# Feed-forward stages' last chunk taken tile by tile, its second weights in the first weights' buffer; first tile's norm diagonal and the attentions' first product started earlier

## The reference, cut to what matters

```python
def rmsnorm(x, g):
    x32 = x.astype(jnp.float32)
    y = x32 * lax.rsqrt(jnp.mean(x32 * x32, axis=-1, keepdims=True) + EPS)
    return (y * g.astype(jnp.float32)).astype(x.dtype)

def swiglu(h, w_in, w_out):            # w_in 1024 x 5632, w_out 2816 x 1024
    gate, up = jnp.split(h @ w_in, 2, axis=-1)
    return (jax.nn.silu(gate) * up) @ w_out

x = x + 0.5 * swiglu(rmsnorm(x, norm_g[layer, 0]), ffn_w_in[layer, 0], ffn_w_out[layer, 0])
hn = rmsnorm(x, norm_g[layer, 1])
x = x + mixer(hn, ...)
x = x + 0.5 * swiglu(rmsnorm(x, norm_g[layer, 2]), ffn_w_in[layer, 1], ffn_w_out[layer, 1])
```

## Time and profile before

| | us |
|---|---|
| median of 3 runs | 2130.42 (2128.65 to 2131.54) |
| the profiled execution, its own time | 2131.05 |
| span of its trace | 2129.7 |
| TensorE busy (matmuls) | 2080.2 |
| VectorE busy | 1197.1 |
| ScalarE busy | 1031.2 |
| mean granted TensorE clock, share of full | 0.994 |

### The profile page before, as it was taken

The page is one execution under the profiler, slowest core; times in us unless marked ns, Lnnn a source line. Parts: engine busy times, 40 slices in busy tenths (PEclk is TensorE's granted clock), DMA queues, the critical chain, the costliest instruction groups (busy, mean ns, idle before and its releaser), DMA issues.

```text
span 2129.7 us, 26075 instructions
## 1 busy us (share of the span) xinstructions
PE 2080.2 (98%) x10491; PEld 1747.2 (82%) x10491; DVE 1197.1 (56%) x1542; ACT 1031.2 (48%) x1359; POOL 71.2 (3%) x113
## 2 busy tenths in 40 slices
PE   8999999999999999999999999999999999989999
PEld 6887988888888878888888879888888787877887
DVE  5445687554654576654465546654555555765454
ACT  6435436444533557643454444444455444764443
POOL 2000000000000000000000000007001000000000
PEclk9999999999999999999999999999999999989999
DMA  7553425655555342565555544586647655115553
GB/s 260 192 193 119 159 97 173 205 180 199 177 193 192 130 158 80 178 203 193 178 178 178 186 169 151 188 248 197 178 135 177 202 184 170 66 52 167 178 179 118
DMA packets 259880, 359.98 MB, mean 169 GB/s; under 512 B 19582, under 2 KB 200234, under 8 KB 259760
## 3 DMA queue, kind: packets, MB, share of 16 engines
q1 hardware_dynamic: 256800, 351.57, 50.3%
q0 software_dynamic: 2016, 4.95, 1.5%
q10 hardware_dynamic: 944, 1.79, 0.3%
HBM read 356.70 MB, written 1.57 MB: 168 GB/s over the span
## 4 chain that ended last, share of the span: by engine, by line
PE 85%; DVE 7%; ACT 5%; issue 1%; DMA 1%; SPq 0%; DVEq 0%; ACTq 0%
PE bank L421 16%; PE bank L423 16%; PE bank L422 16%; PE acc L718 6%; PE acc L719 6%; PE acc L720 6%; PE bank L416 2%; PE bank L417 2%; PE bank L418 2%; DVE w_lo_ L445 2%; ACT w_hi_ L435 2%; PE tr L699 2%; PE acc L748 1%; PE acc L750 1%; PE acc L749 1%
## 5 line engine op out<-in xcount | busy, mean ns | idle before, releaser
L445 DVE TENSOR_TENSOR w_lo_<-raw_in,w_hi_ 128x2048 fp32r<-128x2048 f32 (+1 forms) x333 | 574.5, 1733 | 215.0 <-ACT w_hi_ L435 214.6
L421 PE MATMUL bank<-w_hi_,xt_hi_ 128*128 128x512 f32 x1648 | 658.4, 400 | 3.1 <-DVE xt_lo_ L545 2.4
L423 PE MATMUL bank<-w_hi_,xt_lo_ 128*128 128x512 f32 x1648 | 643.4, 390 | 0.0
L422 PE MATMUL bank<-w_lo_,xt_hi_ 128*128 128x512 f32 x1648 | 642.2, 390 | 0.0
L435 ACT ACTIVATE w_hi_<-raw_in 128x2048 fp32r<-128x2048 f32 (+1 forms) x333 | 481.7, 1461 | 59.5 <-DMA raw_in<-ffn_w_in 30.6
L844 DVE TENSOR_TENSOR wo_lo_<-raw_out,wo_hi_ 128x2048 fp32r<-128x2048 f32 x80 | 183.8, 2298 | 485.3 <-ACT wo_hi_ L798 485.3
L423 PEld LDWEIGHTS bank<-w_hi_,xt_lo_ 128*128 128x128 f32 x1648 | 309.2, 188 | 66.3
L421 PEld LDWEIGHTS bank<-w_hi_,xt_hi_ 128*128 128x128 f32 x1648 | 309.9, 188 | 65.5 <-issue 4.8
L422 PEld LDWEIGHTS bank<-w_lo_,xt_hi_ 128*128 128x128 f32 x1648 | 310.2, 188 | 58.8
L798 ACT ACTIVATE wo_hi_<-raw_out 128x2048 fp32r<-128x2048 f32 x80 | 153.3, 1916 | 370.5 <-PE acc L720 360.9
L718 PE MATMUL acc<-wo_hi_,ht_hi_ 128*128 128x512 f32 x576 | 224.9, 390 | 1.9 <-DVE ht_lo_ L831 1.9
(11 more groups left out here) (379 smaller groups left out, 2094.3 us busy)
## 6 DMA issues: line engine op xcount, KB each, us to landing
raw_in<-ffn_w_in SPq DMA_DIRECT2D x352, 512.0 KB, 4.9
raw_out<-ffn_w_out SPq DMA_DIRECT2D x88, 1024.0 KB, 4.9
raw_in<-hg_w_in SPq DMA_DIRECT2D x16, 1024.0 KB, 5.2
raw_in<-fox_w_in SPq DMA_DIRECT2D x16, 1024.0 KB, 5.3
raw_in<-conv_w_in SPq DMA_DIRECT2D x12, 1024.0 KB, 5.1
raw_in<-hg_w_out SPq DMA_DIRECT2D x4, 1024.0 KB, 5.0
raw_in<-fox_w_out SPq DMA_DIRECT2D x4, 1024.0 KB, 5.1
raw_in<-conv_w_out SPq DMA_DIRECT2D x4, 1024.0 KB, 5.1
```

The lines of the kernel that those rows point to most:

```text
L421: mm(o, xt_hi[:, k, tok], wh[:, par, k, 0:w], start=first, stop=False)
L422: mm(o, xt_hi[:, k, tok], wl[:, par, k, 0:w], start=False, stop=False)
L423: last = mm(o, xt_lo[:, k, tok], wh[:, par, k, 0:w], start=False, stop=end)
L445: dve.e.tensor_tensor(g.piece(g.wl, n, half, k), raw, g.piece(g.wh, n, half, k).bitcast(F32), ALU.subtract).then_inc(g.w_lo, 4 if k is Non ...
```

## The change

The diff, without blank lines and with unchanged context cut:

```diff
+LAST_OUT = {N0[S_FFN[f]] + NCH + 1: f for f in range(7)}
 def act_split(g, act, n, half, k=None):
     act.wait_ge(g.prod, 2 * (n - 2) + 2)
+    if n in LAST_OUT:
+        act.wait_ge(g.acc, 4 * LAST_OUT[n] + 4)
 def pe_turn_x(g, pe, s):
-    for t in range(NT):
+    for t in range(NT if s in BY_K or s not in DIAG else 1):
+def second_tile(g, pe, s, c, t):
+    if (c, t) != (0, 0):
+        return None
+    return lambda k: [pe_turn_half(g, pe, s, 1, half) for half in range(2)] if k == 6 else None
 def act_mixer_turn_x(g, act, s):
-    for t in range(NT):
-        act_squares(g, act, s, t)
-        act_root(g, act, s, t)
+    act_squares(g, act, s, 0)
+    act_root(g, act, s, 0)
+    if s in BY_K:
+        act_squares(g, act, s, 1)
+        act_root(g, act, s, 1)
     act.wait_ge(g.prod, 2 * N0[s])
     for t, k in turn_order(s):
+        if s not in BY_K and (t, k) == (0, 4):
+            act_squares(g, act, s, 1)
+        elif s not in BY_K and (t, k) == (1, 0):
+            act_root(g, act, s, 1)
+def dve_diag(g, dve, s, t):
+    dve_ms(g, dve, s, t)
+    dve.wait_ge(g.rstd, 2 * R[s] + t + 1)
+    dve.e.tensor_scalar(g.diag_[:, t, :], g.ident[:], g.rstd_[:, t:t + 1], None, ALU.mult).then_inc(g.diag, 1)
 def dve_mixer_turn_x(g, dve, s):
-    for t in range(NT):
-        dve_ms(g, dve, s, t)
-        dve.wait_ge(g.rstd, 2 * R[s] + t + 1)
-        dve.e.tensor_scalar(g.diag_[:, t, :], g.ident[:], g.rstd_[:, t:t + 1], None, ALU.mult).then_inc(g.diag, 1)
     for i, (t, k) in enumerate(turn_order(s)):
+        if (t, k) == ((0, 0) if s in BY_K else (1, 0)):
+            dve_diag(g, dve, s, 1)
 def pe_ffn(...):    # chunk 9 as before; chunk 10:
+    c = NCH - 1
+    pe.wait_ge(g.wo_lo, 2 * m_of(f, c) + 2)
+    hi, lo = last_out(g.wh, n0), last_out(g.wl, n0)
+    for t in range(NT):
         for i in range(FC // P):
+            pe.wait_ge(g.ht_lo, 12 * f + c + i + 1)
+            for half in range(2):
+                at, mm, o = i * NT + t, pe.e.matmul, g.accs[2 * t + half][:]
+                mm(o, g.hth[:, at, :], hi[:, 2 * i + half], start=False, stop=False)
+                mm(o, g.hth[:, at, :], lo[:, 2 * i + half], start=False, stop=False)
+                ins = mm(o, g.htl[:, at, :], hi[:, 2 * i + half], start=False, stop=i == 1)
+                if i == 1:
                     ins.then_inc(g.acc, 1)
+def last_out(buffer, n0):
+    return buffer[:, (n0 + NCH - 1) % 2, 0:2 * FC // P]
 def act_ffn(...):
     c = NCH - 1
+    act.wait_ge(g.prod, 2 * (n0 + c) + 2)
+    act.wait_ge(g.landed_out, 16 * (m_of(f, c) + 1))
+    act.e.activation(last_out(g.wh, n0), g.raw_out[:].rearrange("p i (h n) -> p (i h) n", n=CW),
+                     ACT.Copy).then_inc(g.wo_hi, 2)
     for i in range(FC // P):
         act.wait_ge(g.second, 20 * f + 18 + i + 1)
-        act.wait_ge(g.landed_out, 16 * (m_of(f, c) + 1))
-        act.e.activation(g.oh[:, i], g.raw_out[:, i], ACT.Copy).then_inc(g.wo_hi, 1)
 def dve_ffn(...):
+    follow = (lambda: dve_diag(g, dve, S_FFN[f] + 1, 0)) if S_FFN[f] + 1 in DIAG else None
     c = NCH - 1
+    dve.wait_ge(g.wo_hi, 2 * m_of(f, c) + 2)
+    dve.e.tensor_tensor(last_out(g.wl, n0), g.raw_out[:].rearrange("p i (h n) -> p (i h) n", n=CW),
+                        last_out(g.wh, n0).bitcast(F32), ALU.subtract).then_inc(g.wo_lo, 2)
     for i in range(FC // P):
-        dve.wait_ge(g.wo_hi, 2 * m_of(f, c) + i + 1)
-        dve.e.tensor_tensor(g.ol[:, i], g.raw_out[:, i], g.oh[:, i].bitcast(F32), ALU.subtract).then_inc(g.wo_lo, 1)
     for t in range(NT):
         for half in range(2):
             dve.wait_ge(g.acc, 4 * f + a + 1)
             ...
+            if follow and a == 2:
+                follow()
 def pe_fox(g, pe):
-            pe_product(g, pe, n0 + c, t, fx_first(g, c, t), u)
+            pe_product(g, pe, n0 + c, t, fx_first(g, c, t), u, slot=second_tile(g, pe, S_FOX, c, t))
 def pe_nsa(g, pe):
-        pe_product(g, pe, n0, t, g.bank[t], u)
+        pe_product(g, pe, n0, t, g.bank[t], u, slot=second_tile(g, pe, S_NSA, 0, t))
```

More of the change, by code:

```diff
@@ L734, in pe_ffn @@
             second(c - 1)
-    for c in (NCH - 2, NCH - 1):
-        for i in range(FC // P):
[L738 to L751, removed]
-                    ins.then_inc(g.acc, 1)
[L753 to L760, removed]
@@ new lines, in pe_ffn @@
+    c = NCH - 2
+    for i in range(FC // P):
+        pe.wait_ge(g.ht_lo, 12 * f + c + 1)
+        pe.wait_ge(g.wo_lo, 2 * m_of(f, c) + 2)
+        for a in range(4):
+            cols, at = slice(a % 2 * CW, (a % 2 + 1) * CW), i * NT + a // 2
+            mm, o = pe.e.matmul, g.accs[a][:]
+            mm(o, g.hth[:, at, :], g.oh[:, i, cols], start=False, stop=False)
+            mm(o, g.hth[:, at, :], g.ol[:, i, cols], start=False, stop=False)
+            ins = mm(o, g.htl[:, at, :], g.oh[:, i, cols], start=False, stop=False)
+        ins.then_inc(g.second, 1)
+        for t in range(NT):
+            pe.wait_ge(g.h, 22 * f + 2 * (NCH - 1) + t + 1)
+        for t in range(NT):
+            ins = pe.e.transpose(g.tr[i][:, t * P:(t + 1) * P], g.h_[:, t, i * P:(i + 1) * P], g.ident[:])
+        ins.then_inc(g.h_turned, 1)
@@ new lines, in pe_ffn @@
+    c = NCH - 1
+    pe.wait_ge(g.wo_lo, 2 * m_of(f, c) + 2)
+    hi, lo = last_out(g.wh, n0), last_out(g.wl, n0)
+    for t in range(NT):
+        for i in range(FC // P):
+            pe.wait_ge(g.ht_lo, 12 * f + c + i + 1)
[5 more added lines that the diff above has]
+                if i == 1:
+                    ins.then_inc(g.acc, 1)
```

## The result

The changed kernel takes 2137.07 us (median of 7 runs, 2135.97 to 2138.49); the kernel before took 2128.65 us in the same series (7 runs, 2127.23 to 2131.54). The ratio is 1.0039, 95% interval 1.0029 to 1.0048: slower by 8.4 us, a little more than forecast. The profiled execution took 2138.49 us around a span of 2137.1 us, 7.4 us longer than the span before.

The account below looks back on a forecast made before the run. TensorE, busy 2080 of 2130 us, was taken as the bound, with ScalarE and VectorE chains pacing the attentions; -0.4 - 0.45 + 4.0 + 4.0 = +7.2 us on 2130.42 gave 2137.6 us, range 2131 to 2143.

Parts of the forecast that it names:

- T: Moment TensorE is free of the last feed-forward matmul before a mixer; 1806.33 us before the second attention in the earlier trace.
- Part 1: Feed-forward stages, last chunk's second weights in the other buffer: splits covered, gain 0.05 us in each of eight, 0.4 together.
- Part 2: Hand-overs to mixers: tile 0's diagonal products 0.7 us sooner, wait 1.8 to about 1.1; three mixers by k gain 0.15 each.
- Part 3: Both attentions: first product 1.5 us sooner, but last piece of turned input 4.0 us later, all reaching the path in each.
- S: Start of tile 0's diagonal products at the hand-over before the second attention: 1808.27 before, forecast 1807.55 after.
- A wait near 0.8 us: Both attentions, inside the first product after its sixth step: TensorE waits near 0.8 us for tile 1's diagonal.
- No slack: Attentions: next weights' split stands directly behind the pieces in gapless chains, so all 4.0 us reach the path.
- absorbed rival: ScalarE and VectorE catch up within the attention, only TensorE's 1.2 us count, twice: +1.5, 2132 us; chance 0.20.
- w_lo_: First attention: TensorE's wait for split weights was to go up from 3.0 to about 6 us.
- The clock: Half-clock stretches in the attentions may be added or dropped: forecast plus 1.7 to 4.7 us, or as much less.
- the diagonal hides entirely: Hand-overs: tile 0's norm complete before the last matmul, all five waits, 8.9 us, gone, 2121 us; faster's chance 0.10.
- Part 1 failing: Feed-forward stages: the 7th matmul waits in every stage, +2 us on top, inside the range.

Follow-up runs that it names:

- part 3 in the first only: Changed kernel with the second attention's part 3 removed, only the first attention keeping it; 2132.56 us, ratio 1.0009 to the kernel before.
- without part 3: Changed kernel with both tiles' norms and turnings ahead of the first product again in both attentions; 2127.08 us, ratio 0.9990 to the kernel before.
- changed, again: The changed kernel measured once more in a series of its own; 2138.04 us, ratio 1.0040 to the kernel before.
- mean square sooner: Kernel without part 3, with tile 0's mean square behind VectorE's second addition, reciprocal and diagonal behind the third; 2126.03 us, ratio 0.9977 to before.
- slot before step 2: Changed kernel with tile 1's norm ahead of tile 0's pieces and its turning before step 2 instead of 6; 2130.89 us, ratio 1.0007 to before.
- part 3 alone: Kernel before plus only the slot and tile 1's moved squares, root and diagonal in both attentions; 2141.09 us, ratio 1.0050.
- part 1 alone: Kernel before plus only the last chunk tile by tile with second weights in the other buffer; 2128.91 us, ratio 0.9993.
- tile 1's norm ahead of the pieces: Changed kernel with tile 1's squares, root and diagonal ahead of tile 0's pieces, turning still before step 6; 2136.23 us, ratio 1.0028 to before.

## Why the prediction was right, point by point

Distances behind T in us, from the timelines of the profiled executions: the start of tile 0's diagonal products, of the first product and of tile 1's diagonal products, the end of the last piece, and the start of the first feed-forward matmul behind the attention. They are those of the first attention; the last column gives the second attention too, which differs by at most 0.02 in the others (in "part 3 in the first only" it is as in "without part 3").

| kernel | tile 0's diagonal products | first product | tile 1's | last piece | feed-forward behind |
|---|---|---|---|---|---|
| before | 1.94 | 5.66 | 3.88 | 10.25 | 166.23; 134.64 |
| changed | 1.27 | 4.22 | 8.91 | 14.34 | 171.95; 138.60 |
| changed, again | 1.26 | 4.22 | 8.90 | 14.33 | 171.13; 141.86 |
| without part 3 | 1.26 | 5.43 | 3.65 | 9.56 | 165.54; 134.11 |
| mean square sooner | 0.74 | 4.91 | 3.13 | 9.05 | 163.44; 132.60 |
| slot before step 2 | 1.26 | 4.22 | 5.66 | 11.02 | 165.42; 135.06 |
| part 3 in the first only | 1.27 | 4.22 | 8.90 | 14.33 | 168.75; 134.70 |
| part 3 alone | 1.94 | 4.90 | 9.58 | 15.01 | 171.79; 141.98 |
| part 1 alone | 1.94 | 5.66 | 3.88 | 10.25 | 166.22; 134.75 |
| tile 1's norm ahead of the pieces | 1.26 | 4.22 | 8.39 | 13.75 | 168.71; 137.90 |

- **Part 1, -0.4 us.** Its size is below what the times resolve (-0.9 in the medians, interval from -3.4 to +0.4 us). The traces show it: from the first product to the last matmul of the feed-forward stage before the convolution, which has no half clock, the kernels before and with part 3 alone take 184.80 and 184.78 us, the changed one and part 1 alone 184.72. That is nearly 0.1 a stage where I had 0.05. Its splits are covered: the waits for the diagonal with part 1 alone are those of before.
- **Part 2, 0.7 us sooner.** Shown, 0.67 us (1.94 to 1.27), and the waits of 1.1 us are as forecast. Parts 1 and 2 together were put at -2.3 us (-0.4, -0.45, and 0.7 in each attention); the kernel without part 3 gives -2.7, interval -4.0 to -0.2. The 0.15 us of each mixer taken by k is larger in the traces: from the last feed-forward matmul to the first product, at all three such hand-overs, it is 7.07 us before, with part 1 alone and with part 3 alone, and 6.83 or 6.84 in the changed kernel and without part 3. That is 0.24 us each, because tile 1's products start at T + 3.65 (before 3.88) where I had T + 3.72.
- **Part 3, last piece 4.0 us later.** Measured 4.08 and 4.07 us, parts 1 and 2 included. The step held, with two small errors that cancel: tile 0's pieces with tile 1's squares between them took 4.44 us (1813.25 to 1817.69) where I had 4.66, and tile 1's eight pieces 3.37 (1820.89 to 1824.26) where I had 3.13. From the mean square to the diagonal products it was 1.14 us again (1817.69 to 1818.83), and from these to ScalarE's first read 2.06. The last piece came 13.07 us behind S, forecast 13.05.
- **"A wait near 0.8 us" for tile 1's diagonal.** 0.33 by the list of waits; from the last matmul's own end (1818.11 + 0.23) to 1818.83 it is 0.49. Of the missing 0.3 us, 0.22 are the shorter run of tile 0's pieces and 0.1 a sixth step that ended later (S + 7.15, forecast 7.05). This changes nothing in the sum, which goes by the pieces.
- **No slack.** Shown twice over. The chains behind the pieces keep their 7.39 and 13.99 us. And in the three profiles without half clock inside the first attention, the first feed-forward matmul stands 154.39, 154.40 and 154.42 us behind the last piece, though that piece is ready at T + 9.05, 11.02 and 14.33 (mean square sooner, slot before step 2, part 3 in the first only). The absorbed rival fails on its own criterion, a wait of less than about 1 us for split weights at the first product's successor: TensorE waits 0.63 us at its first step and 2.46 at its fifth, where the earlier trace rows had 0.28. Together that is 3.1, as the prediction's "about 3 us".
- **w_lo_, "up from 3.0 to about 6 us".** 5.0 in the changed kernel, both times, and 5.8 in the kernel with the slot in the first attention only, as shown there. The step that failed here is the unstated one that TensorE comes to the later wait at full clock: in the changed kernel it runs a stretch before it at half clock and comes late. The wait is shorter there, and the attention is not.
- **The clock, left out of the sum.** This is the mis-sized term. The first attention lost 5.7 us in the profiles, not 4.0. The rest can be worked out from the executions without half clock inside it. "Mean square sooner" has 163.44 there; add 0.5 for its earlier diagonal, and the kernel without part 3 would be at 163.9 without half clock. It is at 165.54, so its two stretches (near 780 and 801, as in the kernel before) cost 1.6 us, and the kernel before would be at 166.23 - 1.6 = 164.6. "Part 3 in the first only" has 168.75 with none: 4.1 us more, the forecast's 4.0. The changed kernel has 171.95, so its stretches (3.4 us near 758, 6.8 near 806) cost 3.2, and in its second profile (3.4 and 3.4) 2.4. Two kernels check this: with the slot before step 2 and no stretch, 164.6 + 0.8 for the later piece makes 165.4, measured 165.42; with part 3 alone and stretches like the second profile's, 164.6 + 4.75 + 2.4 makes 171.8, measured 171.79. So 5.7 = 4.1 + (3.2 - 1.6). Most of the 3.2 comes with the second stretch: at the third wait for split weights the changed kernel is only 0.8 us behind the execution without half clock (786.80 is 37.91 us behind the last piece, 785.87 there is 37.16), so the stretch near 758 costs 0.8 and the 6.8 us near 806 cost 2.4. The kernel with tile 1's norm ahead of the pieces has one stretch there, near 756, and none near 806: 13.75 + 154.4 makes 168.15, measured 168.71, so it costs 0.6. In the second attention no stretch moved onto the path in the first profile (3.96 us), and one of 10.2 us near 1841 did in the second (141.86 against 138.60, 3.3 us more).
- **The sum.** In the profiled executions: entry to the first attention +0.5 (less than what the waits for loads differ by between executions, so I give it no cause), first attention +5.7, between the attentions -2.6, second attention +4.0, the rest -0.1; together, from the unrounded terms, +7.4. Of the -2.6, 0.5 are part 2 before the convolution and before the keys and values, and 0.2 are part 1. The other 1.9 lie in the feed-forward stage behind the keys and values. There the kernel before has a wait of 1.91 us for turned activations and behind it a half-clock stretch of 3.4 us near 1659; the changed kernel has a wait of 1.58 and no stretch. This is no effect of the change: part 3 alone runs the code of before there, and from the first product to the last matmul it takes 2.7 us less than before. So it is luck that the profiles' +7.4 lies so near the forecast's +7.2: the clock's 1.6 us in the first attention and these 1.9 us nearly cancel. Medians of runs give +8.4 and +8.3. The clock's place can make a microsecond, but which of its stretches recur in the unprofiled runs is not shown. That the forecast time, 2137.6, is only 0.5 us from the measured 2137.07, where its sum is 1.2 too small, is luck too: it started from 2130.42, and beside the changed kernel the one before ran at 2128.65.

The other rivals: that the diagonal hides entirely failed where the prediction put it, at the mean square behind the third addition. The experiment that moves it ahead comes nearest, 2.9 us of waits left of 8.9. Part 1 failing is excluded by its own run.

## What to carry to other kernels

An engine that waits visibly (here TensorE, 1.8 us at each hand-over) may be fed sooner at a price that its list of waits doesn't show: work out when the *last* piece of the feeding engines' run is ready, and look whether their next work stands directly behind it. A slot inside a product must be placed by the engines that consume what it makes: against no slot at all it cost 5.5 us an attention before step 6 (2138.04 against 2127.08, two attentions, half clock included) and 1.9 before step 2 (2130.89); the series differ, but the kernel before has 2129.80 and 2129.76 in them. And a long dependent step (mean square, root, reciprocal, diagonal) can be started where its inputs are ready: one tiny instruction, moved ahead of an addition that it did not need, took the wait from 1.1 to 0.6 us.

## What the runs showed of the hardware

The stretches at half clock are the same in sum in the profiles before and after (23.9 us of the span at the lower level, mean 0.994 in both) and still cost differently. The stretch at 758 slowed matmuls from 0.23 to 0.43 us while TensorE was the chain; of that, 0.83 us came back in a shorter wait (1.90 instead of 2.73) and 0.8 stayed. The 6.8 us near 806 cost 2.4. Over 77 executions in nine series (all kernels but the one before), each compared with its series' mean, the span grows by 1.15 us for each 0.001 of mean clock lost (correlation -0.81). 0.001 of 2130 us is 4.3 us at the lower level, so a microsecond of it goes with 0.27 us of span on the average, where it would be 0.5 if all of it lay on the path. This is about two thirds of the variance between runs of one kernel (0.81 squared), and a reason to compare single profiles by distances inside a stage rather than by their spans.

The stretches do not follow the gaps simply. The wait of 2.46 us in the first attention comes with the lower level in both profiles of the changed kernel, and in those of part 3 alone and of tile 1's norm ahead of the pieces (the stretch begins between 0.5 us before the wait's end and 0.9 us behind it), but not in the kernel with part 3 in the first attention only, whose code up to there and whose two waits of 0.63 and 2.46 us are the changed kernel's. The Trainium skill (TensorE: Matmul & The Clock Gate, Part 1) says that the gate follows how busy TensorE has been recently. Nothing here contradicts it, but by it alone one could not have told which of two equal executions would be slowed.
